# Two modulation chunks are fetched ahead of x and the first norm's sums move between the chunk products; the last two hidden blocks' down-projections are accumulated together in PSUM

## What is computed

```python
mod = jax.nn.silu(c) @ w_ada[l] + b_ada[l]
mod_c = jax.nn.silu(c_ctx) @ w_ada[l] + b_ada[l]
...
h = modulate(rms_norm(x, g_attn[l]), sh_a, sc_a)
hc = modulate(rms_norm(ctx, g_attn[l]), csh_a, csc_a)
# h and hc are then multiplied by the input projection w_in
...
x = x_mid + gt_f * sq_relu_mlp(modulate(rms_norm(x_mid, g_ffn[l]), sh_f, sc_f), w_ff1[l], w_ff2[l])
return rms_norm(x, g_final)     # where the second block begins
```

## Time and profile before

| | |
|---|---|
| device time, median of 3 executions | 2873.0 us (2872.16 to 2876.26) |
| the profiled execution: own time, span of its trace | 2876.15 us, 2874.3 us |
| PE busy | 2650.6 us, 92% of the span |
| DVE busy | 1452.2 us, 51% |
| ACT busy | 1060.4 us, 37% |
| granted PE clock, mean over the span | 0.962 of full speed |

### The profile page before, as it was taken

How to read it: one execution, slowest core, us unless ns; L and a number is a source line. 1 busy time by engine, 2 the same in 40 slices (tenths; PEclk the granted TensorE clock), 3 DMA queues, 4 the chain that set the end, 5 groups by cost and what they waited for, 6 DMA issues and landing times. The chain is left out here.

```text
span 2874.3 us, 35747 instructions
## 1 busy us (share of the span) xinstructions
PE 2650.6 (92%) x14379; PEld 2272.0 (79%) x14379; DVE 1452.2 (51%) x1945; ACT 1060.4 (37%) x1886; POOL 487.7 (17%) x295
## 2 busy tenths in 40 slices
PE   4999869999979999999988999989997999988999
PEld 1777666898767888888877999778887998668887
DVE  4743682433457666666677322257734422236652
ACT  3411443444244333333343222257622222136640
POOL 0102201332000000000001000058800000008740
PEclk9999979999989999999998999999998999999999
DMA  5441101000311111111113132322122113233212
GB/s 227 162 139 50 41 5 52 15 1 1 110 38 52 52 44 52 59 52 43 53 37 113 49 82 53 95 60 49 34 97 113 37 49 86 44 103 73 52 74 88
DMA packets 66545, 189.45 MB, mean 66 GB/s; under 512 B 7888, under 2 KB 26704, under 8 KB 65360
## 3 DMA queue, kind: packets, MB, share of 16 engines
q1 hardware_dynamic: 66384, 187.22, 21.2%
HBM read 146.79 MB, written 16.97 MB: 57 GB/s over the span
## 5 line engine op out<-in xcount | busy, mean ns | idle before, releaser
L2438 DVE SCALAR_TENSOR_TENSOR res<-ps,gates,res 128x1024 f32<-128x1024 f32 x128 | 158.5, 1279 | 106.5 <-PE ps L2567 106.5
L1757 DVE TENSOR_REDUCE da_negmax<-ps 128x1 f32<-128x1040 f32 x136 | 167.8, 1235 | 26.0 <-PE ps L1611 18.8
L2290 ACT ACTIVATE wo_wh<-ff_raw 128x512 fp32r<-128x512 f32 x120 | 75.3, 628 | 283.4 <-DVE ff_raw L2406 114.2
L1742 POOL TENSOR_TENSOR da_E<-da_E,da_F 128x1040 f32<-128x1040 f32 x68 | 163.7, 2407 | 5.7
L1654 PE MATMUL ps<-da_aT,v 128*128 128x128 f32 (+1 forms) x1224 | 159.7, 277 | 0.7 <-ACT qk L1714 0.7
L2567 PE MATMUL ps<-ff_h_hi,wo_wh 128*128 128x512 f32 x512 | 157.8, 389 | 1.4 <-DVE res L2438 1.3
L2567 PE MATMUL ps<-ff_h_lo,wo_wh 128*128 128x512 f32 x512 | 157.6, 389 | 0.0
L2567 PE MATMUL ps<-ff_h_hi,wo_wl 128*128 128x512 f32 x512 | 157.6, 389 | 0.0
L1740 POOL TENSOR_SCALAR da_F<-da_F,da_mixed 128x1040 f32<-128x1040 f32 x68 | 77.0, 1133 | 458.4 <-DVE da_mixed L1768 455.4
L1654 PEld LDWEIGHTS ps<-da_aT,v 128*128 128x128 f32 x1224 | 152.7, 197 | 1.1 <-ACT qk L1714 1.1
L739 POOL MEMSET h_hi<- 128x112 f32 x2 | 0.4, 194 | 797.0 <-POOLq L65 797.0
(11 more groups left out here) (514 smaller groups left out, 6578.9 us busy)
## 6 DMA issues: line engine op xcount, KB each, us to landing
ff_raw<-w_ff SPq DMA_DIRECT2D x48, 512.0 KB, 3.5
ada_w<-w_ada SPq DMA_DIRECT2D x16, 1024.0 KB, 7.0
ff_raw<-w_in SPq DMA_DIRECT2D x20, 512.0 KB, 4.0
pf_raw<-w_in SPq DMA_DIRECT2D x20, 512.0 KB, 3.6
wo_raw<-w_out SPq DMA_DIRECT2D x18, 512.0 KB, 4.5
st_q<-st_q_rounded SPq DMA_DIRECT2D x32, 260.0 KB, 5.3
res<-xT SPq DMA_DIRECT2D x2, 4096.0 KB, 14.3
ada_w<-w_ada SPq DMA_DIRECT2D x4, 2048.0 KB, 26.4
```

The source lines that it names most:

```text
L1742: pool.tensor_tensor(e, e, f, ALU.add).then_inc(s_A, 1)
L1757: dve.tensor_reduce(nm[:, n % 4:n % 4 + 1], window(n), AX.X, ALU.max, negate=True).then_inc(s_nm, 1)
L2290: act.activation(ring(wh, i), src, ACT.Copy).then_inc(s_hi, 1)
L2438: last = dve.scalar_tensor_tensor(out=res[:, m, :], in0=k.ps[:, b:b + 2, :].rearrange("p c w -> p (c w)"), scalar=gate[:, m:m + 1], in1=re ...
```

## The change

Start of the kernel: two chunks of w_ada are fetched ahead of x, x comes in two halves with a semaphore each, then the context, the other two chunks and the two weight tiles. PE multiplies two chunks, then takes the norm's sums, then multiplies the other two. DVE takes the reciprocals before it copies rows. The two weight tiles of the next stage are split in this stage; the next one is told so by `split_first` and skips it.

End of the feed-forward part: the eight down steps are reordered to A0, A1, B0, B1, A2, B2, A3, B3, and the products of B go on adding onto A's in the same PSUM banks. A's output is no longer added to the residual by itself: DVE's update comes once, after B's step, for the sum of both.

```diff
-                for dst, src in load:
-                    sp.dma_start(dst, src).then_inc(s_x, 16)
-                for n in range(ada.FIRST):
+                for n in range(2):
                     ada.fetch(sp, n)
-                fetch_first(sp, k, then)
+                for i, (dst, src) in enumerate(load):
+                    sp.dma_start(dst, src).then_inc(s_x[i], 16)
+                for n in range(2, ada.FIRST):
+                    ada.fetch(sp, n)
+                for i in range(slots):
+                    sp.dma_start(raw[:, i, :], w_rows(i)).then_inc(s_w[i], 16)
...
-                act.wait_ge(s_x, 16 * len(load))
                 for n in range(2 * KD):
+                    if n in (0, KD // 2, KD):
+                        act.wait_ge(s_x[n // (KD // 2)], 16)
                     norm.square(act, n)
                 norm.roots(act, 0)
                 norm.roots(act, 1)
+                for i in range(slots):
+                    act.wait_ge(s_w[i], 16)
+                    act.activation(wh[:, i, :], raw[:, i, :], ACT.Copy).then_inc(s_whi, 1)
...
-                for n in range(ada.FIRST - 1):
+                for n in range(2):
                     ada.multiply(pe, n)
                 norm.sums(pe, 0)
                 norm.sums(pe, 1)
-                ada.multiply(pe, ada.FIRST - 1)
+                for n in range(2, ada.FIRST):
+                    ada.multiply(pe, n)
...
+                norm.reciprocals(dve, 0)
+                norm.reciprocals(dve, 1)
                 for n in range(ada.FIRST - 1):
                     ada.copy_row(dve, n)
-                norm.reciprocals(dve, 0)
+                for i in range(slots):
+                    dve.wait_ge(s_whi, i + 1)
+                    dve.tensor_tensor(wl[:, i, :], raw[:, i, :], wh[:, i, :].bitcast(F32), ALU.subtract)
                 ada.copy_row(dve, ada.FIRST - 1)
-                norm.reciprocals(dve, 1)
...
-    for p in range(1, NP):
+    A, B = NP - 2, NP - 1
+    for p in range(1, B):
         seq += [("up", p, n) for n in range(4 if p < CLASSIC else 7)] + [("down", p - 1, n) for n in range(4)]
-    seq += [("down", NP - 1, n) for n in range(4)]
+    seq += [("up", B, n) for n in range(7)]
+    seq += [("down", *x) for x in ((A, 0), (A, 1), (B, 0), (B, 1), (A, 2), (B, 2), (A, 3), (B, 3))]
...
-    down_base = lambda p, n: 4 * ((p + n) % 2) if p < NP - 1 else 4 * (n % 2)
+    down_base = lambda p, n: 4 * ((p + n) % 2) if p < A else 4 * (n % 2)
...
-                        if n == 1:
+                        if n == 2:
                             join.split_hi(act, 1, raw, wh)
...
-                        update(p, n)
+                        if p != A:
+                            update(p, n)
...
-                        if n == 1:
+                        if n == 2:
                             join.split_lo(dve, 1, raw, wh, wl)
...
-                        if p == NP - 1 and n < 2:
-                            pe.wait_ge(s_ev, 4 * p - 1 + n)
-                        elif p == NP - 1:
+                        if p == A and n >= 2:
+
                             pe.wait_ge(join.s_x, 2 * n - 2)
+                        elif p == B:
+                            pass
...
-                                                       start=(q == 0 and x == 0), stop=(q == 1 and x == 2))
+                                                       start=(p != B and q == 0 and x == 0), stop=(p != A and q == 1 and x == 2))
```

More of the change, by code:

```diff
@@ L203, in adaptive_vectors @@
         ada.open("ada0", w_at, 4, 0, ada.FIRST, 4)
-        s_c, s_bias, s_x, s_silu = k.sem("c_in"), k.sem("bias_in"), k.sem("x_in"), k.sem("silu")
+        s_c, s_bias, s_silu = k.sem("c_in"), k.sem("bias_in"), k.sem("silu")
+        s_x = [k.sem(f"x_in{i}") for i in range(len(load))]
+        name, w_rows, cols, slots = then
+        raw = k.raw[name] = k.sb(f"{name}_raw", [P, slots, cols], k.ring0)
+        wh, wl = k.split[name] = (k.sb(f"{name}_wh", [P, slots, cols], k.ring0 + 8192, F32R),
+                                  k.sb(f"{name}_wl", [P, slots, cols], k.ring0 + 16384, F32R))
+        s_w, s_whi = [k.sem(f"{name}_first{i}") for i in range(slots)], k.sem(f"{name}_first_hi")
         norm.open_stats()
@@ L2251, in source @@
             kind, p, n = x
+            if kind == "down" and p == B:
+                return (raw[:, 1, n * H:(n + 1) * H], (s_r1, 16 * NP)) if n < 2 else (down_raw[:, (n - 2) * H:(n - 1) * H], (s_r2, 16 * NP))
             if kind == "down":
                 return (down_raw[:, n * H:(n + 1) * H] if n < 2 else raw[:, 0, (n - 2) * H:(n - 1) * H]), \
-                       ((s_r2, 16 * (p + 1)) if n < 2 else (s_r0, 16 * (2 * p + 2 if p < NP - 1 else 2 * NP - 1)))
+                       ((s_r2, 16 * (p + 1)) if n < 2 else (s_r0, 16 * (2 * p + 2)))
             if p < CLASSIC:
@@ L2268, in _ @@
                 sp.dma_start(down_raw[:], row(2 * NP)).then_inc(s_r2, 16)
-                for p in range(NP):
-                    sp.wait_ge(s_lo, count(last0(p + 1) if p + 1 < NP else ("down", p - 1, 3)))
+                for p in range(B):
+                    sp.wait_ge(s_lo, count(last0(p + 1)))
                     sp.dma_start(raw[:, 0, :], row(2 * NP + 2 * p + 1)).then_inc(s_r0, 16)
@@ L2275, in _ @@
                         sp.dma_start(raw[:, 1, :], row(2 * p + 5)).then_inc(s_r1, 16)
-                    if p + 1 < NP:
-                        sp.wait_ge(s_lo, count(("down", p, 1)))
-                        sp.dma_start(down_raw[:], row(2 * NP + 2 * p + 2)).then_inc(s_r2, 16)
+                    else:
+                        sp.wait_ge(s_lo, count(last1(B)))
+                        sp.dma_start(raw[:, 1, :], row(2 * NP + 2 * B)).then_inc(s_r1, 16)
+                    sp.wait_ge(s_lo, count(("down", p, 1)))
+                    sp.dma_start(down_raw[:], row(2 * NP + 2 * p + (2 if p < A else 3))).then_inc(s_r2, 16)
                     if p + 2 < NP:
@@ L2281, in _ @@
                         sp.dma_start(raw[:, 0, :], row(2 * p + 4)).then_inc(s_r0, 16)
[L2282 removed]
+                join.join_fetch(sp, s_lo, {1: count(("down", B, 1)), 0: count(("down", A, 3))}, raw)
             @block.scalar
@@ L3472, in project @@
         last.then_inc(freed, 1)
-    gemm(nc, k, "ina", rows(d["w_ina"]), 8, KD, XH, XL, cx, norm=n1, preloaded=True, then=("inb", rows(d["w_inb"]), KD * P, 2),
+    gemm(nc, k, "ina", rows(d["w_ina"]), 8, KD, XH, XL, cx, norm=n1, preloaded=True, split_first=k.split["ina"], then=("inb", rows(d["w_inb"]), KD * P, 2),
          evac_act=project,
```

3 lines of the change are left out of this document (1 added, 2 removed).

## The result

| | before | changed |
|---|---|---|
| median, 5 executions each, taken in turn on one chip | 2873.2 us (2872.16 to 2876.26) | 2857.95 us (2854.11 to 2859.98) |
| the profiled execution: span | 2874.3 us | 2856.2 us |

The ratio is 0.9942 with a 95% interval of 0.9931 to 0.9953: faster by 0.6%, 15 us by the medians, where 16.8 us were forecast. The interval allows 13.5 to 19.8 us. The median was forecast at 2856.2 us.

What follows compares the result with a forecast made beforehand. PE works 92% of the span, so gains lie where it idles: its late start in the first stage, DVE at the feed-forward end. 8.0 + 8.8 = 16.8 us takes the median from 2873.0 to 2856.2; range 2853 to 2862.

Steps and rivals of the forecast that it cites:

- The first stage's order: First stage: with two chunks ahead of x, PE's chunks end at 56.75 instead of 60.96, 4.2 us earlier (2.1 to 4.9).
- Bias: End of first stage: the context's reciprocal comes earlier and no longer holds the bias, 0.4 us.
- Weight split: Head of second stage: DVE's first scaling can start at once instead of after the split, 3.4 us.
- The cover on DVE: First stage: DVE's moved work fits under the last chunk, ending near 55.9, 0.8 us before that chunk ends.
- Sum of the start: First stage in all: 4.2 + 0.4 + 3.4 = 8.0 us, between 5.9 and 8.7.
- The end of the feed-forward part: Join: tile 6's update starts at 1496.65 instead of 1505.46, 8.8 us earlier; bounds 7.8 and 9.9.
- The spare time ahead of B's step 2: Feed-forward end: DVE's earlier B groups are done by 1487.4, before B2 is ready at 1488.29, 0.9 us to spare.
- Stages in between have no clock of their own: Between the edited places: every later transfer is issued after a wait on the engines and shifts with them.
- x late: Rival, first stage: both halves of x come at about 31.0, the start gives 3.6 us, 2860.6 in all; chance 0.10.
- Transfers side by side: Rival, first stage: big transfers share the engines evenly, x comes near 45.7, kernel 2.3 us slower, 2875.3; chance 0.02.
- The join's chain unmoved: Rival, join: DVE's groups run past 1488.29, the 8.8 us shrink, at nothing 2865; chance 0.05.
- Less than the change says: Rival, start and join: gains partly taken back, with both stages half lost 2864.6 to 2868; chance 0.06.

Runs made afterwards that it cites:

- e2_end_only: The kernel before with only the feed-forward part's edits, the start unchanged; median 2865.31 us, ratio to before 0.9968.
- e3_x_first: The changed kernel with x, still in halves, and the context fetched ahead of all four chunks; 2859.43 us, ratio 0.9948.
- e8_x_whole: The changed kernel with x fetched in one 4 MB transfer, still behind two chunks; 2861.72 us in one execution.
- e4_split_later: The changed kernel with the two preloaded weight tiles split at the head of the second stage again; 2859.23 us in one execution.
- e1_start_only: The kernel before with only the first stage's edits, the feed-forward part unchanged; median 2863.98 us, ratio to before 0.9968.
- e5_order_only: The changed kernel with the new down-step order, but A and B in PSUM banks and updates of their own; 2862.52 us in one execution.
- e6_fill_start: The changed kernel with six unused products in PE's pause before the first norm's sums; 2857.39 us in one execution.
- e7_fill_both: The changed kernel with six unused products before the first norm's sums and 26 ahead of the join's sums; 2855.68 us, ratio 0.9925.

## Why the prediction was right

**The first stage's order, 4.2 us.** Measured: 60.96 - 55.90 = 5.1, which is 0.2 above the upper bound of 4.9. The other traces say that the term was sized too small by more than this pair shows. Five traces have this order, both halves and no filling; their chunks end at 54.22 to 55.90 (the first profile is the latest of them), those of the kernel before and of e2_end_only at 60.96 and 60.40. That makes 4.5 to 6.7 us. The mechanism held in all its parts: chunks in front, a pause for the norm's sums (5.5 forecast, 5.75 measured), x's sums at the lower clock (3.5 and 3.78). Every event came 0.8 to 1.2 us earlier than forecast: the first chunk at 15.23 instead of 16.0, the halves at 25.07 and 30.10 instead of 26 and 31, the sums at 36.46 instead of 37.65. The landing of the first chunk was extrapolated back from landings of the old order, and was put 0.8 too late for this trace. In the nine traces with a chunk in front PE starts at 14.09 to 15.23. With 2 MB of x in front (e3_x_first) ACT's first square, which waits for them, starts at 16.23, as the extrapolation has it: a chunk as the first transfer lands 1 to 2 us sooner. Why was not tried. e3_x_first and e8_x_whole show that order and halves make the term.

**Bias, 0.4 us.** From the turn's start to the bias it was 1.53 us before and 1.26 now: 0.3. What is left is the wait for PE's turn.

**Weight split, 3.4 us.** Measured 2.8 across the two kernels and 2.9 by e4_split_later. This term was mis-sized: DVE's beginning in the new stage, which the split had partly covered, was counted as saved.

**The cover on DVE, 0.8 us,** was 1.84: the context's sum was complete at 40.50 instead of 41.75, and all of DVE's work followed.

**Sum of the start:** 8.0 forecast, 8.16 measured, of which 0.3 lie ahead of the stage's first large transfer (SPq's first one was issued at 6.54 instead of 6.82). The errors of the terms went against one another, +0.9 and -0.7: that 8.0 and 8.16 lie so close is luck. The four traces with the whole of the start's change and no filling (the changed kernel twice, e1_start_only, e5_order_only) have the first scaling at 58.05 to 59.70, the kernel before and e2_end_only at 67.86 and 67.30. The start is worth 7.6 to 9.8 us, and the bound of 8.7 was too low.

**The end of the feed-forward part, 8.8 us.** The lead over the kernel before grew from 11.59 us at the third down step's update to 20.43 at tile 6's: 8.84. By step: the updates of B's steps came 7.01 and 16.32 us after the first (7.65 and 16.32 forecast), tile 6's 24.65 (24.68). The spare time ahead of B's step 2 was 1.67 us, not 0.9. A2 and A3 show no wait for DVE in PE's timeline from the last up steps to the end of the last down step, as argued. e5_order_only adds what the prediction didn't separate: 5.4 from the order, 3.4 from the accumulation.

**The stages between.** "Stages in between have no clock of their own" did not hold for a pair of traces. The lead was 8.16 us at the first scaling and 11.59 at the third down step's update, and of the 20.37 us at the join's sums 18.1 were left at the end. So 16.9 us were gained in the edited places and 1.2 in others. The control is e2_end_only: its code is that of the kernel before up to the last blocks of the feed-forward part, and it still took 1400.37 us from the first scaling to the third down step's update (67.30 to 1467.67), the kernel before 1404.11 (67.86 to 1471.97). Its two rows:

```profile
67.30 2.48 DVE L753 SCALAR_TENSOR_TENSOR n_z<-res,a,n_rstd 128x1024 f32<-128x1024 f32 x2
...
1467.67 2.48 DVE L2445 SCALAR_TENSOR_TENSOR res<-ps,gates,res 128x1024 f32<-128x1024 f32 x2 [4.00 <-PE ps L2576]
```

All of the 3.7 us are there before the feed-forward part begins: its first scaling (`ffn_in_kept`) comes 755.56 us behind the first one in e2_end_only and 759.23 in the kernel before. e1_start_only, whose start is changed, took 1404.13 us to the third down step. In the ten traces with the new order of the down steps it is 1400.3 to 1404.0 us, and e3_x_first (1403.99) and e8_x_whole (1403.62) are among them: the stretch wanders by nearly 4 us, and the changed start is not what shortens it. That the granted clock behind PE's many pauses makes it wander is argued from PE's busy time, not shown piece by piece. It follows that the forecast median, 1.8 us below the first measured one and 1.1 above the second, came closer than a sum of such terms can be trusted to come.

**The rivals.** x late: the squares began at 25.07, with the first half's bytes; it falls. Transfers side by side: it falls with the same row, and e8_x_whole, where the whole of x is waited for, has its first square 14.88 us behind PE's first product instead of 9.84: later by the 5.0 us of the second half's bytes. The join's chain unmoved: it falls by 15.11 to 6.33. Less than the change says: half a gain in each stage would have left e1_start_only and e2_end_only near 4 us each; they gave 9.5 and 8.1.

## What to carry to other kernels

Look for the stage's bound on both sides of the place to be edited: at the start the late first operand of PE mattered, not its amount of work, and putting another engine's data behind it paid although PE then waited 5.75 us for that engine's chain, because it had begun 13.3 us sooner. Where a slower engine follows PE step by step at the end of a stage, order the steps so that its work is spread out and none of it is left over when the last piece becomes ready, and let PSUM do its additions. Before reading a few us of difference in an untouched stretch as an effect, take a second trace of one of the kernels.

## What the runs showed that was not expected

**An issue that waits.** With two chunks ahead of x, SPq's issue of the context took 6.93 us in the changed kernel, where the same transfer took 0.65 before. In the eight other traces with this order it took 5.94 to 6.81 us. Each time it ended some 0.6 us after PE's first product, which starts when the first chunk has landed (15.78 and 15.23 in the changed kernel). With x in front (e3_x_first, e2_end_only and the kernel before) no large issue took over 2.1 us, though 13 MB had been issued by 13.1 us and the first of them landed at 16.2 at the earliest. In e8_x_whole, with three large transfers ahead instead of four, the issue took 6.54 us all the same. So neither the number of transfers nor the bytes issued ahead explain it alone. It cost nothing here, because the bytes ahead kept the DMA engines busy (the next landings stayed 5.0 us apart) and PE never waited for the third chunk. What holds the issue wasn't tried.

**The order of landing.** The large transfers of the first stage, six in the kernel before and seven in the changed one, landed in the order of issue in both orders, 4.9 to 5.0 us for 2 MB. The Trainium skill, "DMA: Bandwidth & Descriptors", section "Queues, rings and completion order", warns that completion is not first-in-first-out for one issuing engine; no run here shows an exception to the order.

**The clock behind a short pause.** The same two pieces of code, a pause of 2.12 us with products on both sides, kept the upper level once (e6_fill_start) and lost it once (e7_fill_both), at a price of 1.7 us. A single trace doesn't tell whether a pause is harmless.
